# P·V of the sampled tokens with the cached values as the stationary operand, two matmuls a step, in place of one block and a turn back

## The chip, the cores and the metric

One core of one Trainium2 chip runs the whole program. The metric is the device time of one execution in microseconds; lower is better. The engines are TensorE (PE, with its weight loads shown apart as PEld), VectorE (DVE), ScalarE (ACT), GpSimd (POOL) and the DMA queues of SyncE (SP).

## What is computed

One decoder layer, in fp32, for 1024 prompt tokens and 8 sampled tokens, each sampled token with its own cache of keys and values. The mixer has 12 attention heads in 3 groups with dilations 1, 4 and 16. What the change touches is the attention of the sampled tokens. For each of the 8 sequences, each group and each of its 4 heads of 64 columns:

```python
kgat = jnp.take(kc, idxc, axis=1)          # up to 128 strided rows of the cache, and the own key
vgat = jnp.take(vc, idxc, axis=1)
s = jnp.einsum('nthd,ntkhd->nthk', qg, kgat).astype(jnp.float32) * SCALE
lse = jax.nn.logsumexp(s, axis=-1)
p = jnp.exp(s - lse[..., None])
outs.append(jnp.einsum('nthk,ntkhd->nthd', p.astype(vg.dtype), vgat))
```

The three groups are then merged by softmax weights; the kernel does this by one softmax over all three groups' scores of a token and head. The result (`o_a`, 256 columns a token) is projected with `w_proj_attn` and gated by `sigmoid(gate_a)`.

## The kernel before

**Tiling.** All activations are kept transposed, features on partitions and tokens along the free axis: 1032 tokens (`NT`), cut in three column tiles `tg` = 0, 1, 2 of 344 (`TG`). A fp32 product is made of three fast ones: both operands are split in a high and a low part, and `product3` (lines 474 to 479) does high·high, high·low and low·high. A *unit* is one 128 x 1024 block of weights: `unit` runs, for each `tg`, one `job` of 8 values of k with three matmuls each, 24 matmuls of 344 columns. `job` can take an `aside`: functions called just before a given k, which put foreign instructions into TensorE's order.

**Weights.** SP loads each unit's weights to `w_raw`; ACT copies the high part (`split`, L1005, to `w_hi`) once the unit two back is used up, DVE subtracts to get `w_lo` (L1500), and TensorE waits for `w_lo`.

**The stage in question.** In stage `ga` TensorE runs six units j = 0..5 of the gate A projection; ACT takes the tanh of each bank (L1235). The sampled tokens' attention runs between them: scores on DVE in j = 1 to 3, softmax in j = 3, then

- `sample_turn`, aside in (j, tg) = (4, 1) at k = 2: turns the probabilities `ssr` to `psA`; DVE copies them to `spT` (L1760 to L1762, semaphore `s_ptc`). `spT` holds, for each group, keys on partitions and 32 columns, one for each (sequence, head).
- `sample_pv`, aside in (4, 2) at k = 0: waits for `s_ptc` and for the 24 tiles of cached values `cv` (one for each sequence and group; 128 keys on partitions for the first two groups and 32 for the third, 256 columns: 4 heads of 64). For each tile one fp32 matmul takes **spT as the stationary operand** (32 columns) and streams 256 columns of `cv`; all 32 rows come out, although only the 4 of one sequence are wanted. Four sequences lie in four column strips of 32 of one bank (`psB`, `psC`). The own value rows (`svt`, 8 rows) go to `psA`. 27 matmuls, then `s_pv`.
- DVE copies the three results out (L1765 to L1767, `s_ov`).
- `sample_back`, aside in (5, 0) at k = 4: six transposes back to features on partitions (`s_ot`); DVE picks the wanted columns and adds the own part in 8 small operations (L1780) into the last 8 columns of `oaT`, each counting up `s_oa`.

**After it.** ACT waits for `s_oa` = 8 after the tanh of (5, 1) (L1242) and makes `oa_hi` of tile 2 (`oa_high(2)`, L1227), DVE `oa_lo` of tile 2 (`oa_low(2)`, L1722) and then the `w_lo` of the next unit. Stage `pa` (projection of `oaT`, 2 units of 2 values of k) waits for `oa_s` by tile; DVE multiplies its result by the gate (L1793, L1805). SP waits for `s_oa` (L414) before it loads `xs` and `grow` over the scratch space.

Of the kernel before, what the change touches and what calls it, by code (L numbers as in the profile page):

```python
# [12 lines left out]
ALU = mybir.AluOpType  # L13
ACT = mybir.ActivationFunctionType
F32 = mybir.dt.float32
# [4 lines left out]
P = 128  # L20
D = 1024
KD = D // P
SEQ = 1024
NS = 8
NT = SEQ + NS
TG = NT // 3
HD = 64
SLOTS = 4
GROUPS = 3
# [8 lines left out]
CKEYS = (128, 128, 32)  # L38
# [78 lines left out]
def build(nc, A, O):  # L117
    ctx = ExitStack()
    sem = lambda name: ctx.enter_context(nc.semaphore(name))
# [6 lines left out]
    X = R4 + RB  # L126
# [3 lines left out]
    def at(name, shape, dt, off):  # L130
        n = 4 if dt in (F32, F32R, I32) else 2
        for s in shape[1:]:
            n *= s
        assert off + n <= nc.sbuf_usable_end, (name, off, n)
        return nc.alloc_sbuf_tensor_at(name, shape, dt, offset=off), off + (n + 31) // 32 * 32

    with ctx:
# [4 lines left out]
        h_hi, _ = at("h_hi", [P, KD, NT], F32R, R[0])  # L142
        h_lo, _ = at("h_lo", [P, KD, NT], F32R, R[1])
        xn, _ = at("xn", [P, 8, D], F32, R[0])
# [3 lines left out]
        mb, _ = at("mb", [P, KD, NT], F32, R[2])  # L148
        m_hi, _ = at("m_hi", [P, KD, NT], F32R, R[2])
        a_hi, _o = at("a_hi", [P, FG, NT], F32R, R[2])  # L150
        a_lo, _ = at("a_lo", [P, FG, NT], F32R, _o)
        d_hi = [at(f"d_hi{i}", [P, 8 * P], F32R, R[2] + 2 * NT * 4 + 4096 * i)[0] for i in range(2)]
        d_lo = [at(f"d_lo{i}", [P, 8 * P], F32R, R[2] + (FG + 2) * NT * 4 + 4096 * i)[0] for i in range(2)]
        uv, _ = at("uv", [P, 8, NT], F32, R[3])
        ob_hi, _o = at("ob_hi", [P, 4, NT], F32R, R[3])
        ob_lo, _ = at("ob_lo", [P, 4, NT], F32R, _o)
        m_lo, _ = at("m_lo", [P, KD, NT], F32R, R[4])
        y2, _ = at("y2", [P, KD, NT], F32, R[4])
# [17 lines left out]
        oaT, _o = at("oaT", [P, 2, NT], F32, R[3])  # L176
# [36 lines left out]
        assert _o <= XEND and XEND - 3648 >= VTO, (_o, XEND)  # L213

        kq, _o = at("kq", [P, 2, 256], F32, X)
        ov, _ = at("ov", [P, 2, 256], F32, X)
        qz, _o = at("qz", [P, 2, 3, NS, 2], F32, _o)
        sst, _o = at("sst", [P, 2, 96], F32, _o)
        ssr, _o = at("ssr", [32, 320], F32, _o)
# [67 lines left out]
        sk_in = [sem(f"k_cache_landed{i}") for i in range(8)]  # L287
        sq_in = [sem(f"s_query_landed{i}") for i in range(3)]
        sv_in = sem("v_cache_landed")
        s_ov, s_ot = sem("s_pv_copied"), sem("s_pv_turned")  # L290
        s_qz, s_kq, s_sc, s_self, s_sst, s_rows, s_ssr, s_exp, s_pn, s_pt, s_ptc, s_pv, s_oa, s_nt, s_nc, s_out = [
            sem("s_" + s) for s in ("queries", "k_times_q", "scores", "self", "scores_out", "rows", "rows_out",
                                    "exp", "probs", "probs_turned", "probs_out", "pv", "o_out", "new_turned", "new_out",
# [33 lines left out]
        def _(sp):  # L327
# [83 lines left out]
            for i in range(2):  # L411
                load_ga(U0["gc"] + i, 6 + i)

            sp.wait_ge(s_oa, 8)  # L414
            sp.wait_ge(s_out, 48)
            sp.dma_start(xs[0:NS, :], x_s).then_inc(xr_in[8], 16)
            sp.dma_start(grow[:], A["g_mix_post"][0:1, :].broadcast_to([P, D])).then_inc(row_in, 16)
# [50 lines left out]
        def _(pe):  # L468
            mm = nc.tensor.matmul

            def turn(out, in_):
                k = in_.shape[0]
                return nc.tensor.transpose(out, in_, ident[0:k, 0:k])  # L473
# [320 lines left out]
                    ins = turn(psA[0:NS, 96 + 32 * g:128 + 32 * g], ssr[:, 288 + 8 * g:296 + 8 * g])  # L794
                ins.then_inc(s_pt, 1)

            def sample_pv():


                pe.wait_ge(s_ptc, 3)  # L800
                pe.wait_ge(sv_in, 16 * 24)
                for q, ps in ((0, psB), (1, psC)):
                    for g in range(GROUPS - 1):
                        for c in range(4):
                            mm(ps[32 * c:32 * c + 32, 0:256], spT[:, g, :], cv[:, 3 * (4 * q + c) + g, :],
                               start=(g == 0), stop=False)
                for q, ps in ((0, psB), (1, psC)):
                    for c in range(4):
                        mm(ps[32 * c:32 * c + 32, 0:256], spT[0:32, 2, :], cv[0:32, 3 * (4 * q + c) + 2, :],
                           start=False, stop=True)  # L810
                for g in range(GROUPS):
                    ins = mm(psA[0:32, 256:512], spT[0:NS, 3 + g, :], svt[:, g, 1, :], start=(g == 0), stop=(g == 2))
                ins.then_inc(s_pv, 1)

            def sample_back():

                pe.wait_ge(s_ov, 3)
                for q in range(2):
                    for p in range(2):
                        c = 256 * q + P * p  # L820
                        turn(psT[0][:, c:c + P], ov[:, q, P * p:P * p + P])
                for p in range(2):
                    ins = turn(psT[1][:, 32 * p:32 * p + 32], ssr[:, P * p:P * p + P])
                ins.then_inc(s_ot, 1)

            ASIDE_GA = {(4, 1): {2: sample_turn}, (4, 2): {0: sample_pv}, (5, 0): {4: sample_back}}

            for j in range(6):
                u = U0["ga"] + j

                def after(b, tg, j=j):
                    sample_step(j, tg)
                    merge_step(1, j, tg)
                unit(u, M0["ga"] + j, u % 2, 8, h_hi, h_lo, after=after,
                     aside=lambda tg, j=j: ASIDE_GA.get((j, tg)))
            for j in range(2):
                u = U0["pa"] + j
                unit(u, M0["pa"] + 4 * j, u % 2, 2, oa_hi, oa_lo, before=lambda tg: pe.wait_ge(oa_s, tg + 1))
# [158 lines left out]
        def _(act):  # L997
# [232 lines left out]
            for j in range(6):  # L1230
                for tg in range(3):
                    if (j, tg) == (4, 0):
                        act.wait_ge(s_kq, 24)
                    act.wait_ge(full[tg], M0["ga"] + j + 1)
                    fn(ga[:, j, tgc[tg]], bank[tg][:, 0:TG], ACT.Tanh, scale=0.5).then_inc(free[tg], 1)  # L1235
                    if (j, tg) == (3, 2):
                        act.wait_ge(s_ssr, 1)
                        fn(ssr[:, 0:312], ssr[:, 0:312], ACT.Exp, scale=SCALE, bias=stat[0:32, 53:54],
                           accum_out=stat[0:32, 54:55]).then_inc(s_exp, 1)
                    merge_in(1, j, tg)  # L1240
                    if (j, tg) == (5, 1):
                        act.wait_ge(s_oa, 8)  # L1242
                        oa_high(2)
                split_in(U0["ga"], 0, 0, j, M0["ga"] + j + 1)
                if j == 4:
                    oa_high(0)
                    oa_high(1)
# [242 lines left out]
        def _(dve):  # L1490
            v = nc.vector
# [249 lines left out]
            for j in range(6):  # L1741
                for kk in range(max(8 * j - 8, 0), min(8 * j, 24)):
                    if kk == 2:
                        merge_sum(1)
                    k_scores(kk)
                if j == 3:
                    dve.wait_ge(s_self, 1)
                    v.tensor_copy(sst[0:NS, 1, :], psB[0:NS, 0:96]).then_inc(s_sst, 1)
                    dve.wait_ge(s_rows, 1)
                    dve.wait_ge(masks_s, 2)  # L1750
                    st.link(v.tensor_copy(ssr[:, 0:288], psC[0:32, 0:288]))
                    st.link(v.tensor_tensor(ssr[:, 288:312], psC[0:32, 288:312], smask[:].rearrange("p g n -> p (g n)"), ALU.add))
                    st.link(v.reduce_max(stat[0:32, 55:56], ssr[:, 0:312], mybir.AxisListType.X))
                    v.tensor_scalar(stat[0:32, 53:54], stat[0:32, 55:56], -SCALE, None, ALU.mult).then_inc(s_ssr, 1)
                    dve.wait_ge(s_exp, 1)
                    st.link(v.reciprocal(stat[0:32, 56:57], stat[0:32, 54:55]))
                    v.tensor_scalar(ssr[:, 0:312], ssr[:, 0:312], stat[0:32, 56:57], None, ALU.mult).then_inc(s_pn, 1)
                    lo_in(U0["ga"], 0, 0, j)
                    dve.wait_ge(s_pt, 1)
                    v.tensor_copy(spT[:, 0:2, :].rearrange("p g n -> p (g n)"), psA[:, 0:64]).then_inc(s_ptc, 1)  # L1760
                    v.tensor_copy(spT[0:32, 2, :], psA[0:32, 64:96]).then_inc(s_ptc, 1)
                    v.tensor_copy(spT[0:NS, 3:6, :].rearrange("p g n -> p (g n)"), psA[0:NS, 96:192]).then_inc(s_ptc, 1)  # L1762
                if j == 4:
                    dve.wait_ge(s_pv, 1)
                    v.tensor_copy(ov[:, 0], psB[:, 0:256]).then_inc(s_ov, 1)  # L1765
                    v.tensor_copy(ov[:, 1], psC[:, 0:256]).then_inc(s_ov, 1)
                    v.tensor_copy(ssr[:, 0:256], psA[0:32, 256:512]).then_inc(s_ov, 1)  # L1767
                if j == 5:
                    oa_low(0)
                    oa_low(1)  # L1770
                    dve.wait_ge(s_ot, 1)
                    st.link(v.tensor_copy(sst[:, 0, 0:64], psT[1][:, 0:64]))
                    for p in range(2):
                        for q in range(2):
                            for e in range(2):

                                hd, at_n = slice(HD * e, HD * e + HD), SEQ + 4 * q
                                first = P * (2 * q + p) + 16 * q + 2 * p + e
                                own = 32 * p + 16 * q + 2 * p + e
                                v.tensor_tensor(oaT[hd, p, at_n:at_n + 4], psT[0][hd, first:first + 109:36],  # L1780
                                                sst[hd, 0, own:own + 13:4], ALU.add).then_inc(s_oa, 1)
                    oa_low(2)
                if j != 3:
                    lo_in(U0["ga"], 0, 0, j)
# [393 lines left out]
```

## Time and profile before

| | us |
|---|---|
| device time, median of the runs shown | 1582.84 |
| lowest of them | 1582.22 |
| the profiled execution | 1582.84 |
| its span, first to last instruction | 1580.9 |
| TensorE matmuls busy in the span | 1538.7 (97%) |
| TensorE weight loads busy | 1494.2 (95%) |
| DVE busy | 543.8 (34%) |
| ACT busy | 492.0 (31%) |
| POOL busy | 141.4 (9%) |

The profile is of one execution. Matmuls overlap: a dense one of 344 columns lasts 0.32 us in its row but the next one starts after 0.157 us, so the distance between starts tells more than the durations. A timeline row merges neighbouring instructions of one kind ("x16") and gives the start of the first and the time until the end of the last. "psB<-cv,spT 128*32 128x256" reads: output to `psB`, moving operand `cv` of 128 partitions x 256 elements, stationary operand `spT` of 128 rows * 32 columns. The granted clock is that of TensorE as a share of 2.4 GHz.

### The profile page before, as it was taken

To read this page: it belongs to the slowest core of one execution; us is meant where nothing else is said; L and a number is where in the kernel's file an instruction comes from. 1 tells how busy PE (TensorE), PEld (TensorE's weight loads), DVE (VectorE), ACT (ScalarE), POOL (GpSimd) and SP (SyncE) were. 2 spreads that over 40 slices of the span, in tenths; PEclk is the share of its full clock that TensorE was granted. 3 is DMA by queue.
4 is the path that set the end of the run, shared out by engine and by line. 5 is a ranking of instruction groups with operands and counts; after the bars stand their busy time and mean duration, and the time that the engine had idled before them with its cause. 6 is when DMAs were issued, how large, how long until landed. Compare 5 with 4: busy or idle time off the path is not lost.

```text
span 1580.9 us, 23134 instructions
## 1 busy us (share of the span) xinstructions
PE 1538.7 (97%) x9881; PEld 1494.2 (95%) x9881; DVE 543.8 (34%) x1016; ACT 492.0 (31%) x951; POOL 141.4 (9%) x172
## 2 busy tenths in 40 slices
PE   5999999999999999999999999999999999999995
PEld 5999999899998999998789999999999999999995
DVE  6104551332214336654652231132122213122236
ACT  5215543443224422336662111211111211121123
POOL 1000000000000025240001101100100110010014
PEclk9999999999999999999999999999999999999998
DMA  6111112100112025134422111111111111111102
GB/s 201 41 53 41 41 41 83 41 28 28 41 41 84 28 83 187 55 107 167 141 80 80 41 54 41 54 41 47 48 52 43 43 51 46 48 42 53 41 27 108
DMA packets 127169, 101.50 MB, mean 64 GB/s; under 512 B 4632, under 2 KB 114208, under 8 KB 127072
## 3 DMA queue, kind: packets, MB, share of 16 engines
q1 hardware_dynamic: 124208, 91.67, 18.7%
q0 software_dynamic: 2720, 7.89, 1.6%
q8 instruction: 75, 1.23, 0.3%
q10 hardware_dynamic: 144, 0.52, 0.1%
q14 instruction: 22, 0.18, 0.0%
HBM read 92.34 MB, written 7.73 MB: 63 GB/s over the span
## 4 chain that ended last, share of the span: by engine, by line
PE 92%; DVE 4%; POOL 1%; issue 1%; DMA 1%; ACT 1%; SPq 0%; ACTq 0%; DVEq 0%; POOLq 0%
PE bank L894 31%; PE bank L477 11%; PE bank L479 10%; PE bank L478 10%; PE bank L902 5%; PE bank L904 5%; PE bank L903 5%; PE psT L473 3%; PE psC L664 1%; PE bank L864 1%; PE bank L863 1%; PE bank L862 1%; PE psA L664 1%; POOL cv L2098 1%; PE psB L624 1%
## 5 line engine op out<-in xcount | busy, mean ns | idle before, releaser
L894 PE MATMUL bank<-f_hi,w_hi 128*128 128x384 f32 (+1 forms) x1056 | 338.6, 321 | 0.2 <-DVE w_lo L1500 0.2
L894 PE MATMUL bank<-f_hi,w_lo 128*128 128x384 f32 (+1 forms) x1056 | 337.8, 320 | 0.0
L894 PE MATMUL bank<-f_lo,w_hi 128*128 128x384 f32 (+1 forms) x1056 | 337.4, 320 | 0.0
L477 PE MATMUL bank<-h_hi,w_hi 128*128 128x344 f32 x1008 | 331.4, 329 | 1.6 <-DVE h_lo L1513 1.4
L1500 DVE TENSOR_TENSOR w_lo<-w_raw,w_hi 128x1024 fp32r<-128x1024 f32 x138 | 169.0, 1225 | 473.7 <-ACT w_hi L1424 226.6
L479 PE MATMUL bank<-h_hi,w_lo 128*128 128x344 f32 x1008 | 322.1, 320 | 0.0
L478 PE MATMUL bank<-h_lo,w_hi 128*128 128x344 f32 x1008 | 321.9, 319 | 0.0
L894 PEld LDWEIGHTS bank<-f_hi,w_hi 128*128 128x128 f32 x1056 | 198.5, 188 | 0.8 <-DVE w_lo L1500 0.5
L894 PEld LDWEIGHTS bank<-f_lo,w_hi 128*128 128x128 f32 x1056 | 198.5, 188 | 0.0
L894 PEld LDWEIGHTS bank<-f_hi,w_lo 128*128 128x128 f32 x1056 | 198.5, 188 | 0.0
L477 PEld LDWEIGHTS bank<-h_hi,w_hi 128*128 128x128 f32 x1008 | 190.0, 189 | 6.3 <-issue 5.0
L478 PEld LDWEIGHTS bank<-h_lo,w_hi 128*128 128x128 f32 x1008 | 189.7, 188 | 0.0
L479 PEld LDWEIGHTS bank<-h_hi,w_lo 128*128 128x128 f32 x1008 | 189.7, 188 | 0.0
L904 PE MATMUL bank<-a_hi,w_lo 128*128 128x384 f32 (+1 forms) x480 | 153.8, 320 | 0.0
L903 PE MATMUL bank<-a_lo,w_hi 128*128 128x384 f32 (+1 forms) x480 | 153.5, 320 | 0.0
L902 PE MATMUL bank<-a_hi,w_hi 128*128 128x384 f32 (+1 forms) x480 | 153.5, 320 | 0.0
L2124 POOL TENSOR_TENSOR a_lo<-sg,a_hi 128x384 fp32r<-128x384 f32 (+1 forms) x66 | 61.6, 934 | 776.7 <-ACT a_hi L1339 776.7
L1424 ACT ACTIVATE w_hi<-w_raw 128x1024 fp32r<-128x1024 f32 x58 | 61.0, 1052 | 202.6 <-PE bank L904 202.6
L1876 DVE TENSOR_TENSOR y<-y,bank 128x384 f32<-128x384 f32 (+1 forms) x120 | 61.1, 510 | 114.6 <-PE bank L904 114.6
L1339 ACT ACTIVATE a_hi<-sg 128x384 fp32r<-128x384 f32 (+1 forms) x66 | 32.5, 492 | 204.9 <-DVE sg L1868 204.9
L902 PEld LDWEIGHTS bank<-a_hi,w_hi 128*128 128x128 f32 x480 | 90.3, 188 | 0.0
L904 PEld LDWEIGHTS bank<-a_hi,w_lo 128*128 128x128 f32 x480 | 90.1, 188 | 0.0
(412 smaller groups left out, 1845.9 us busy)
## 6 DMA issues: line engine op xcount, KB each, us to landing
w_raw<-in_w_in SPq DMA_DIRECT2D x42, 512.0 KB, 3.9
w_raw<-in_w_out SPq DMA_DIRECT2D x24, 512.0 KB, 3.8
w_raw<-in_w_gate SPq DMA_DIRECT2D x23, 512.0 KB, 3.9
w_raw<-in_w_up SPq DMA_DIRECT2D x23, 512.0 KB, 4.0
w_raw<-in_w_down SPq DMA_DIRECT2D x22, 512.0 KB, 3.5
xin<-in_x_prompt SPq DMA_DIRECT2D x8, 512.0 KB, 7.7
xn<-in_x_prompt SPq DMA_DIRECT2D x8, 512.0 KB, 4.8
out_y_prompt<-xn SPq DMA_DIRECT2D x8, 512.0 KB
```

What stands on the lines that cost most here:

```text
L473: return nc.tensor.transpose(out, in_, ident[0:k, 0:k])
L477: mm(out[:, 0:TG], w_hi[par][:, ws], hi[:, k, tgc[tg]], start=first, stop=False)
L478: mm(out[:, 0:TG], w_hi[par][:, ws], lo[:, k, tgc[tg]], start=False, stop=False)
L479: return mm(out[:, 0:TG], w_lo[par][:, ws], hi[:, k, tgc[tg]], start=False, stop=last)
L894: ins = mm(out[:, 0:NG[tg]], w[par][:, ws], x[tg][:, k, :], start=(k == 0 and w is w_hi and x is f_hi), stop=(k == KD - 1 and w is w_lo))
L902: mm(out[:, 0:NG[tg]], hi[:, ws], a_hi[:, k, tgf[tg]], start=(k == 0), stop=False)
L903: mm(out[:, 0:NG[tg]], hi[:, ws], a_lo[:, k, tgf[tg]], start=False, stop=False)
L904: ins = mm(out[:, 0:NG[tg]], lo[:, ws], a_hi[:, k, tgf[tg]], start=False, stop=(k == kc - 1))
L1424: fn(w_hi[j % 2][:], w_raw[j % 2][:], ACT.Copy).then_inc(w_hi_s, 1)
L1500: v.tensor_tensor(w_lo[par][:], w_raw[par][:], w_hi[par][:].bitcast(F32), ALU.subtract).then_inc(w_lo_s, 1)
L1876: v.tensor_tensor(part, part, src[:, 0:NG[tg]], ALU.add).then_inc(free[tg], 1)
L2124: g_.tensor_tensor(a_lo[:, j, tgf[tg]], sg[:, tgf[tg]], a_hi[:, j, tgf[tg]].bitcast(F32), ALU.subtract).then_inc(ff_l, 1)
```

## The change

The roles are swapped. `sample_pv(c)` is now one of 27 steps of two fp32 matmuls (p = 0, 1: the two halves of 128 of the 256 value columns). In each, 128 columns of `cv` or `svt` are the **stationary** operand, and the moving operand is only the wanted probabilities: 2 columns (the two heads of that half) for a cache tile, 16 for the own rows. The result comes out with features on partitions, all in the first 32 columns of `psB`, so nothing has to be turned back. One start flag (the first own-row matmul) and one stop flag (the last) bound the accumulation.

The steps lie one at each k: the three own-row steps in (4, 1) at k = 5, 6, 7; the 24 cache steps at k = 0 to 7 of (4, 2), (5, 0) and (5, 1). `sample_turn` stays at (4, 1), k = 2. `sample_back`, the tile `ov` and the semaphores `s_ov` and `s_ot` go. DVE waits for `s_pv` in j = 5, between `oa_low(1)` and `oa_low(2)`, and copies twice from `psB` to `oaT`; `s_oa` ends at 2.

```diff
-            sp.wait_ge(s_oa, 8)
+            sp.wait_ge(s_oa, 2)
...
-            def sample_pv():
-                pe.wait_ge(s_ptc, 3)
-                pe.wait_ge(sv_in, 16 * 24)
-                for q, ps in ((0, psB), (1, psC)):
-                    for g in range(GROUPS - 1):
-                        for c in range(4):
-                            mm(ps[32 * c:32 * c + 32, 0:256], spT[:, g, :], cv[:, 3 * (4 * q + c) + g, :],
-                               start=(g == 0), stop=False)
-                for q, ps in ((0, psB), (1, psC)):
-                    for c in range(4):
-                        mm(ps[32 * c:32 * c + 32, 0:256], spT[0:32, 2, :], cv[0:32, 3 * (4 * q + c) + 2, :],
-                           start=False, stop=True)
-                for g in range(GROUPS):
-                    ins = mm(psA[0:32, 256:512], spT[0:NS, 3 + g, :], svt[:, g, 1, :], start=(g == 0), stop=(g == 2))
-                ins.then_inc(s_pv, 1)
-
-            def sample_back():
-                pe.wait_ge(s_ov, 3)
-                for q in range(2):
-                    for p in range(2):
-                        c = 256 * q + P * p
-                        turn(psT[0][:, c:c + P], ov[:, q, P * p:P * p + P])
-                for p in range(2):
-                    ins = turn(psT[1][:, 32 * p:32 * p + 32], ssr[:, P * p:P * p + P])
-                ins.then_inc(s_ot, 1)
-
-            ASIDE_GA = {(4, 1): {2: sample_turn}, (4, 2): {0: sample_pv}, (5, 0): {4: sample_back}}
+            def sample_pv(c):
+                if c == 0:
+                    pe.wait_ge(s_ptc, 3)
+                for p in range(2):
+                    if c < GROUPS:
+                        out = psB[:, 16 * p:16 * p + 16].rearrange("k (n e) -> k n e", e=2)
+                        w = spT[0:NS, 3 + c, :].rearrange("k (n s) -> k n s", s=4)[:, :, 2 * p:2 * p + 2]
+                        mm(out, svt[:, c, 1, P * p:P * p + P], w, start=(c + p == 0), stop=False, skip_group_check=True)
+                        continue
+                    if c == GROUPS and p == 0:
+                        pe.wait_ge(sv_in, 16 * 24)
+                    kk = c - GROUPS
+                    n, g = kk // 3, kk % 3
+                    ck = CKEYS[g]
+                    ins = mm(psB[:, 16 * p + 2 * n:16 * p + 2 * n + 2], cv[0:ck, kk, P * p:P * p + P],
+                             spT[0:ck, g, 4 * n + 2 * p:4 * n + 2 * p + 2], start=False,
+                             stop=(kk == 23 and p == 1), skip_group_check=True)
+                    if kk == 23 and p == 1:
+                        ins.then_inc(s_pv, 1)
+
+            PV_AT = [(4, 1, 5), (4, 1, 6), (4, 1, 7)] + [(j, tg, k) for j, tg in ((4, 2), (5, 0), (5, 1)) for k in range(KD)]
...
-                        act.wait_ge(s_oa, 8)
+                        act.wait_ge(s_oa, 2)
...
-                if j == 4:
-                    dve.wait_ge(s_pv, 1)
-                    v.tensor_copy(ov[:, 0], psB[:, 0:256]).then_inc(s_ov, 1)
-                    v.tensor_copy(ov[:, 1], psC[:, 0:256]).then_inc(s_ov, 1)
-                    v.tensor_copy(ssr[:, 0:256], psA[0:32, 256:512]).then_inc(s_ov, 1)
                 if j == 5:
                     oa_low(0)
                     oa_low(1)
-                    dve.wait_ge(s_ot, 1)
-                    st.link(v.tensor_copy(sst[:, 0, 0:64], psT[1][:, 0:64]))
-                    for p in range(2):
-                        for q in range(2):
-                            for e in range(2):
-                                hd, at_n = slice(HD * e, HD * e + HD), SEQ + 4 * q
-                                first = P * (2 * q + p) + 16 * q + 2 * p + e
-                                own = 32 * p + 16 * q + 2 * p + e
-                                v.tensor_tensor(oaT[hd, p, at_n:at_n + 4], psT[0][hd, first:first + 109:36],
-                                                sst[hd, 0, own:own + 13:4], ALU.add).then_inc(s_oa, 1)
+                    dve.wait_ge(s_pv, 1)
+                    for e in range(2):
+                        hd = slice(HD * e, HD * e + HD)
+                        v.tensor_copy(oaT[hd, :, SEQ:NT], psB[hd, 0:32].rearrange("d (p n e) -> d p n e", p=2, e=2)[:, :, :, e]
+                                      ).then_inc(s_oa, 1)
                     oa_low(2)
```

## Rows read from the trace of the kernel before

**Rows 1.** The page: chain that ended last, by engine and by line

```profile
PE 92%; DVE 4%; POOL 1%; issue 1%; DMA 1%; ACT 1%; SPq 0%; ACTq 0%; DVEq 0%; POOLq 0%
PE bank L894 31%; PE bank L477 11%; PE bank L479 10%; PE bank L478 10%; PE bank L902 5%; PE bank L904 5%; PE bank L903 5%; PE psT L473 3%; PE psC L664 1%; PE bank L864 1%; PE bank L863 1%; PE bank L862 1%; PE psA L664 1%; POOL cv L2098 1%; PE psB L624 1%
```

**Rows 2.** Timeline of TensorE, `sample_pv`: start us, us, engine, line, operation

```profile
628.45 0.31 PE L479 MATMUL bank<-h_hi,w_lo 128*128 128x344 f32 x1
...
629.16 1.07 PE L805 MATMUL psB<-cv,spT 128*32 128x256 f32 x16 [0.40 <-DMA cv<-in_cache_win]
...
633.56 0.32 PE L478 MATMUL bank<-h_lo,w_hi 128*128 128x344 f32 x1
```

**Rows 3.** Timeline of TensorE around `sample_back`

```profile
638.90 0.32 PE L479 MATMUL bank<-h_hi,w_lo 128*128 128x344 f32 x1
...
640.09 0.32 PE L478 MATMUL bank<-h_lo,w_hi 128*128 128x344 f32 x1
```

**Rows 4.** Timeline, three transposes between dense matmuls

```profile
293.10 0.32 PE L479 MATMUL bank<-h_hi,w_lo 128*128 128x344 f32 x1
...
293.26 0.49 PE L473 MATMUL psT<-ident,pr 128*128 128x128 f32 x3
...
293.75 0.32 PE L478 MATMUL bank<-h_lo,w_hi 128*128 128x344 f32 x1
```

**Rows 5.** Timeline, twelve fp32 passes of the prompt's P·V

```profile
296.59 0.31 PE L479 MATMUL bank<-h_hi,w_lo 128*128 128x344 f32 x1
...
296.75 0.78 PE L664 MATMUL psA<-vtok,prT 128*128 128x64 f32 x6
...
298.30 0.32 PE L478 MATMUL bank<-h_lo,w_hi 128*128 128x344 f32 x1
```

**Rows 6.** Timeline around L775, then L775 by source line

```profile
611.60 0.32 PE L479 MATMUL bank<-h_hi,w_lo 128*128 128x344 f32 x1
...
611.85 0.46 PE L775 MATMUL psB<-qz,sqkv 128*8 128x16 f32 x12
...
612.24 0.42 PE L477 MATMUL bank<-h_hi,w_hi 128*128 128x344 f32 x1
...
L775 PE MATMUL psB<-qz,sqkv x12: 176/176/183, 611.8 to 612.1; 128*8 128x16 f32 x12
```

**Rows 7.** Weight loads: L624, `vw` by tile, then their timeline

```profile
L624 PEld LDWEIGHTS psB<-qk x64: 187/187/188, 286.8 to 550.0; 64*128 64x128 f32 x64
...
L473 PEld LDWEIGHTS psA<-ident,vw x4: 133/136/137, 234.3 to 234.5; 8*128 8x128 f32 x4
...
234.33 0.32 PEld L473 LDWEIGHTS psA<-ident,vw 8*128 8x128 f32 x4 [0.21 <-issue]
```

**Rows 8.** Timeline of DVE, TensorE and ACT up to the next stage

```profile
626.01 0.24 DVE L1762 COPY spT<-psA 8x96 f32<-8x96 f32 x1
...
627.19 0.32 PE L477 MATMUL bank<-h_hi,w_hi 128*128 128x344 f32 x1
...
645.79 0.46 ACT L1235 ACTIVATE ga<-bank 128x344 f32<-128x344 f32 x1 [3.31 <-PE bank L479]
...
646.15 0.77 ACT L1227 ACTIVATE oa_hi<-oaT 128x688 fp32r<-128x688 f32 x1
...
649.92 1.05 ACT L1005 ACTIVATE w_hi<-w_raw 128x1024 fp32r<-128x1024 f32 x1
...
651.00 1.22 DVE L1500 TENSOR_TENSOR w_lo<-w_raw,w_hi 128x1024 fp32r<-128x1024 f32 x1 [3.18 <-ACT w_hi L1005]
```

**Rows 9.** Busy us by stretch with clock (PEclk), then timeline of TensorE there

```profile
core 0: us, PE busy (x) PEld busy (x) DVE busy (x) ACT busy (x) POOL busy (x), PEclk, DMA share, GB/s
...
17.00:24.00 7.00, 3.95 (x20) 3.60 (x21) 6.82 (x12) 5.73 (x12) 1.28 (x3) 0.55 0.97 291
...
23.24 0.49 PE L478 MATMUL bank<-h_lo,w_hi 128*128 128x344 f32 x1
...
23.53 0.49 PE L479 MATMUL bank<-h_hi,w_lo 128*128 128x344 f32 x1
```

More of the change, by code:

```diff
@@ L215, in build @@
         kq, _o = at("kq", [P, 2, 256], F32, X)
-        ov, _ = at("ov", [P, 2, 256], F32, X)
         qz, _o = at("qz", [P, 2, 3, NS, 2], F32, _o)
@@ L289, in build @@
         sv_in = sem("v_cache_landed")
-        s_ov, s_ot = sem("s_pv_copied"), sem("s_pv_turned")
         s_qz, s_kq, s_sc, s_self, s_sst, s_rows, s_ssr, s_exp, s_pn, s_pt, s_ptc, s_pv, s_oa, s_nt, s_nc, s_out = [
@@ L828, in _, with pv_aside @@
+            PV_AT = [(4, 1, 5), (4, 1, 6), (4, 1, 7)] + [(j, tg, k) for j, tg in ((4, 2), (5, 0), (5, 1)) for k in range(KD)]
+            def pv_aside(j, tg):
+                steps = {k: (lambda c=c: sample_pv(c)) for c, (a, b, k) in enumerate(PV_AT) if (a, b) == (j, tg)}
+                if (j, tg) == (4, 1):
+                    steps[2] = sample_turn
+                return steps
             for j in range(6):
@@ L834, in _ @@
                 unit(u, M0["ga"] + j, u % 2, 8, h_hi, h_lo, after=after,
-                     aside=lambda tg, j=j: ASIDE_GA.get((j, tg)))
+                     aside=lambda tg, j=j: pv_aside(j, tg))
             for j in range(2):
```

## The prediction, made before the changed kernel ran

> **What bounds the kernel now.** I read the page's chain first: 92% of the span is TensorE work and its leading lines are the matmul streams [rows 1]. So an edit is worth what it adds to or takes from TensorE's own instruction stream, unless it makes TensorE wait. Then the timeline of TensorE around the sampled tokens' P·V. The dense stream (`product3`, 344 columns) starts a matmul every 0.157 us: from 633.56 to 638.90 there are 34 intervals [rows 2, 3]. I price each interruption of that stream by one rule: take the slot at which the next dense matmul was due, take the start of the *second* dense matmul after the interruption, subtract, and subtract one slot of 0.157. The second is used because the first one after an interruption is itself followed 0.24 to 0.27 us later, not 0.157.
>
> `sample_pv`: last dense start 628.45, so the next was due at 628.61; second start afterwards 633.56 [rows 2]. 633.56 − 628.61 − 0.157 = 4.79 us, of which 0.40 is a wait for the cached values. `sample_back`: last dense start 638.90, due 639.06, second afterwards 640.09 [rows 3]: 0.87 us. Together **5.66 us of TensorE** on the path.
>
> **Removed.** 27 matmuls of `sample_pv`, 6 transposes, three DVE copies out of PSUM, one more copy and eight tiny adds. Only the TensorE part counts: nothing waits for DVE's part but the chain to `oa_hi(2)`, costed below. Credit 5.66 us. The 0.40 us wait is rightly in the credit: the new own-row groups come before the wait for the cache, so TensorE gets there later than 628.61 by about 2 us, after the values have landed.
>
> **Added: how many instructions.** 27 groups (3 own-row, 24 cache) of two fp32 matmuls. An fp32 matmul appears as two passes with a weight load each: L805 is 8 matmuls on `psB` and 16 records [rows 2]. So 54 matmuls are 108 passes, 4 in a group, and every pass loads a stationary tile 128 columns wide, where before it was 32. The moving side shrinks from 256 columns to 2 (16 for own rows). Streaming becomes nothing; loading becomes everything. The question is what four 128-wide loads cost when wedged between dense matmuls.
>
> **Price of a group without change of row tile** (16 groups, 128 keys). Nearest rows: three transposes with 128-wide loads: due 293.26, second dense start 293.75, loss 0.33 us [rows 4]. Twelve fp32 passes in the prompt's P·V, 128-wide loads, only 64 moving columns: due 296.75, second dense start 298.30, loss 1.39 us [rows 5]. Slope (1.39 − 0.33)/9 = 0.118 us per load, so four cost 0.33 + 0.118 = **0.45 us**. 16 × 0.45 = 7.2 us.
>
> **Price of a group that changes the row tile** (8 groups of 32 keys and 3 of 8 own rows). A 64-row, 128-wide load still lasts 187 ns [rows 7], so I let fewer rows save nothing. But a change of tile shape costs extra. The twelve passes of L775 (8-column loads) were due at 611.757 and began at 611.85, so 0.09 us on entry. Their last pass starts at 611.85 + 0.46 − 0.176 = 612.134, and the dense stream resumes at 612.24, 0.106 us later [rows 6], although nothing in that pass takes 0.1 us; I round that to 0.12 for leaving. 0.45 + 0.09 + 0.12 = **0.66 us**. 11 × 0.66 = 7.26 us.
>
> The Trainium skill, "TensorE: Matmul & The Clock Gate", section "LDWEIGHTS (loading the stationary operand)", says that a load lasts its column count divided by 1.2, in ns, whatever the rows. By that rule alone, with 107 ns a load, 27 groups of four would cost an estimated 11.6 us, net +5.9 us; the 0.21 us for changing the tile shape isn't in it. The rows agree with the rule on the load and add the shape change, and I go by the rows. The rule speaks against this change: it makes the 128-wide operand the stationary one.
>
> **Waits that move.** The own-row groups now need `spT` at (4,1), k=5; `sample_pv` needed it only at (4,2), k=0. The last copy to `spT` ends at 626.25 and TensorE is at k=5 at 627.19 [rows 8]: 0.9 us to spare, no stall; `sample_turn` stays where it was. If that cover were gone TensorE would stall by the excess alone.
>
> The result is now complete only in the last k of (5,1) instead of at 633. Queued behind on DVE: two copies (under 0.25 us each, as L1762), `oa_low(2)`, then `lo_in(5)`; on ACT, behind `wait_ge(s_oa, 2)`: `oa_high(2)`, the tanh of (5,2), the w_hi split; on SP nothing earlier than `xs` and `grow`, which follow weight loads already held back by `w_lo`. The pass that signals is issued 3 dense matmuls (0.47 us) before (5,1) ends. ACT does not look at `s_oa` before it has done the tanh of (5,1), 0.46 us, which in turn waits for that job's end [rows 8]. Two copies fit in 0.47 + 0.46 = 0.93 us, so `oa_high(2)` still follows the tanh directly, as it did at 646.15. `oa_low(2)` follows within 2 us, while (5,2) keeps TensorE busy 24 × 0.157 = 3.8 us, and tile 2 of unit pa is wanted a further 0.94 later. Nothing added. If the copies were a microsecond late, `oa_low(2)` still is in time.
>
> What follows is tied to TensorE: the w_hi split at 649.92 waits for the end of (5,2), the w_lo at 651.00 for it, the products after that [rows 8]. So a delay of TensorE reaches the end in full, with no slack to swallow it.
>
> **Sum.** +7.2 + 7.26 − 5.66 = +8.8 us. The profiled execution lasted 1582.84 us with a span of 1580.9 and is the median of the runs shown, so the forecast is 1582.84 + 8.8 = **1591.6 us**, +0.56%: slower, but within 2% (about what a measurement of this kernel can tell from no change).
>
> **Bounds.** Low: every group at the transposes' 0.33 us, 27 × 0.33 = 8.9, net +3.3, 1586.1 us. High: every group pays the shape change and 0.05 more for the second column range, 27 × 0.71 = 19.2, net +13.5, 1596.3 us.
>
> **Rivals.**
> *A, the forecast* (loads of 107 to 118 ns bound each pass): 70%.
> *B, fast loads.* Four transposes of 8 rows had 128-wide loads and finished four loads within 0.32 us, (0.32 − 0.13)/3 = 0.063 apart [rows 7]. If few moving columns allow that pace, a group costs 0.25, with shape change 0.46: 16 × 0.25 + 11 × 0.46 = 9.1, net +3.4, 1586.2 us. Against: those were transposes, and the fp32 matmuls of [rows 5] did not reach it. 10%.
> *C, not slower.* The pass follows the moving width, not the stationary one. L775 with 16 moving columns runs at (0.46 − 0.176)/11 = 0.026 us per pass [rows 6]; at that pace a group costs 0.10, with shape change 0.31: 16 × 0.10 + 11 × 0.31 = 5.0, net −0.6, 1582.2 us. It decides if a group costs under 5.66/27 = 0.21 us. For: the moving side does shrink to 2 columns. Against: L775's stationary side was 8 wide too, and [rows 4, 5] have the same 128-wide load but 128 and 64 moving columns at nearly one pace. 5%.
> *D, no overlap.* With 2-column passes each load waits until the matmul before it has left the array: 0.106 us (as between the end of L775 and the dense stream) on top of 0.118, four times: 0.90 us a group, 24.3, net +18.6, 1601.5 us. Against: L775's small passes show no such gap. 8%.
> *E, the clock falls.* The groups cut TensorE's dense share from (4,2) to (5,1) to 0.47 of 0.92 to 1.13 us. In the start phase with TensorE busy 3.95 of 7 us the granted clock was 0.55, toward the 1.2 GHz level, and a dense matmul took 0.29 us [rows 9]. If all 24 steps ran so: 24 × 3 × 0.13 = 9.4 us more for the dense part alone, 1601 us. Against: before that fall the engine had been truly idle, and here it is loading all the time. 7%. The Trainium skill, "TensorE: Matmul & The Clock Gate", Part 1, makes the low level the default that activity lifts; whether loads with two columns count as activity no row here shows.
>
> **Range.** 1585.5 to 1597: it holds A within its bounds and B (80%), and leaves out C, D and E. A alone: 1588 to 1596. Faster by over 2%: 0.01. Slower by over 2% (above 1614.5) would need D and E together: 0.02. Within 2%: 0.97.
>
> **What would show it.** TensorE between (4,1) k=5 and the end of (5,1) longer by 14.5 us minus the two blocks taken out; groups of 4 passes with starts 0.11 apart; group loss 0.45 at 128 keys and 0.66 at 32; no TensorE wait for `spT` or the cache; `oa_high(2)` following ACT's tanh directly; clock 1.00 in 625 to 665. Wrong if a group costs under 0.3 or over 0.8 us, if the dense matmuls slow to 0.29, or if a stage after 670 changes length.

## The result, and the profile after

The changed kernel takes 1592.72 us (median of 5 runs, 1592.64 to 1593.27) against 1582.84 us for the median shown before. The ratio to the kernel before is **1.0057, 95% interval 1.0045 to 1.0069**: slower by 0.57%, within 2%. The kernel before ran five times beside it, at 1582.22, 1582.84, 1584.68, 1584.70 and once 1905.31 us, and the ratio leaves the last one out and goes by the median of the other four, 1583.8 us. So the change costs 8.9 us by that median and 9.9 us by the one shown before; the forecast was +8.8, 1591.6 us.

The page of the changed kernel (span; matmuls and weight loads, DVE, ACT, POOL busy; chain that ended last, by engine):

```profile
span 1590.3 us, 23220 instructions
...
PE 1549.5 (97%) x9929; PEld 1504.5 (95%) x9929; DVE 542.0 (34%) x1006; ACT 492.3 (31%) x951; POOL 141.5 (9%) x172
...
PE 94%; DVE 3%; ACT 1%; issue 1%; DMA 1%; SPq 0%; POOL 0%; ACTq 0%; DVEq 0%
```

The span grew from 1580.9 to 1590.3 us, TensorE's busy time by 10.8 us; the chain is still TensorE's.

Where the 9.4 us lie can be read off without any pricing rule. The stretch from `sample_turn` to the first matmul of stage `pa` holds the same dense matmuls in both kernels. Its ends, before and then after:

```profile
625.31 0.42 PE L473 MATMUL psA<-ident,ssr 32*128 32x32 f32 x6
...
649.37 0.32 PE L477 MATMUL bank<-oa_hi,w_hi 128*128 128x344 f32 x1
```

```profile
625.16 0.42 PE L471 MATMUL psA<-ident,ssr 32*128 32x32 f32 x6
...
658.68 0.32 PE L475 MATMUL bank<-oa_hi,w_hi 128*128 128x344 f32 x1
```

It took 24.05 us and now takes 33.52, **9.47 us more**. From the first matmul of `pa` to the end of the span it is 931.5 us before and 931.6 after: everything that follows kept its length.

Timeline of TensorE in the changed kernel (lines are two lower than before: the dense stream is L475 to L477). First a step with a tile of 128 keys, then one with 32 keys:

```profile
630.51 0.32 PE L477 MATMUL bank<-h_hi,w_lo 128*128 128x344 f32 x1
...
630.67 0.50 PE L810 MATMUL psB<-spT,cv 128*128 128x2 f32 x4
...
631.28 0.32 PE L476 MATMUL bank<-h_lo,w_hi 128*128 128x344 f32 x1
...
632.36 0.31 PE L477 MATMUL bank<-h_hi,w_lo 128*128 128x344 f32 x1
...
632.61 0.60 PE L810 MATMUL psB<-spT,cv 32*128 32x2 f32 x4
...
633.40 0.32 PE L476 MATMUL bank<-h_lo,w_hi 128*128 128x344 f32 x1
```

Read by the rule of the prediction. 128 keys: due 630.667, second dense start 631.28, loss 0.46 us. 32 keys: due 632.517, second dense start 633.40, loss 0.73 us. The 0.09 us between due and start of the first pass (632.61) is the entry into another row tile, as in [rows 6]. The own-row steps:

```profile
626.88 0.32 PE L477 MATMUL bank<-h_hi,w_lo 128*128 128x344 f32 x1
...
627.12 0.61 PE L803 MATMUL psB<-spT,svt 8*128 8x16 f32 x4
...
627.94 0.32 PE L476 MATMUL bank<-h_lo,w_hi 128*128 128x344 f32 x1
```

Due 627.037, second dense start 627.94: 0.75 us. Over all 27 steps of the trace the means are 0.741 us (own rows), 0.726 (32 keys) and 0.448 (128 keys): 3 x 0.741 + 8 x 0.726 + 16 x 0.448 = **15.2 us added**, where [rows 2, 3] gave 5.66 us back: 9.5 us net, as the stretch above shows. The number of passes was as counted (24 cache tiles x 2 halves x 2 passes; count, ns min/median/max, starts, shapes):

```profile
L810 PE MATMUL psB<-spT,cv x96: 165/251/267, 630.7 to 654.2; 128*128 128x2 f32 x64, 32*128 32x2 f32 x32
```

The hand-over to the next stage: DVE's two copies, then ACT's tanh, `oa_high(2)` and the next w_hi split:

```profile
L1767 DVE COPY oaT<-psB x2: 167/172/178, 654.4 to 654.6; 64x16 f32<-64x16 f32 x2
...
655.11 0.46 ACT L1233 ACTIVATE ga<-bank 128x344 f32<-128x344 f32 x1 [7.72 <-PE bank L477]
...
655.47 0.77 ACT L1225 ACTIVATE oa_hi<-oaT 128x688 fp32r<-128x688 f32 x1
...
659.23 1.05 ACT L1003 ACTIVATE w_hi<-w_raw 128x1024 fp32r<-128x1024 f32 x1
```

DVE copies at 654.4 and 654.6, ACT starts its own tanh at 655.11 and `oa_high(2)` directly after it at 655.47, as at 646.15 in [rows 8]. Before, the w_hi split that follows unit (5,2) started at 649.92 [rows 8]; now it starts at 659.23, 9.3 us later.

Busy us and granted clock over the 27 steps, changed kernel (columns as in [rows 9]; the clock is the last but two):

```profile
627.10:655.00 27.90, 27.90 (x191) 25.58 (x191) 3.14 (x5) 3.65 (x6) 0.00 (x0) 1.00 0.11 34
```

It stays at the 2.4 GHz level through all 27 steps. The 24 executions of the changed kernel on record lie between 1591.91 and 1593.53 us, with a granted clock of 0.995 or more over the whole span, so none of them lost the clock here.

### The profile page after: what moved, and what is told of

It is laid out like the page before. It is cut to its first block, busy times and chain, and to the rows that moved or that the text cites. A ratio compares the mean times of both kernels' runs of the same rounds, so it can differ in the third digit from the quotient of the medians.

```text
span 1590.3 us, 23220 instructions
## 1 busy us (share of the span) xinstructions
PE 1549.5 (97%) x9929; PEld 1504.5 (95%) x9929; DVE 542.0 (34%) x1006; ACT 492.3 (31%) x951; POOL 141.5 (9%) x172
## 4 chain that ended last, share of the span: by engine, by line
PE 94%; DVE 3%; ACT 1%; issue 1%; DMA 1%; SPq 0%; POOL 0%; ACTq 0%; DVEq 0%
PE bank L892 31%; PE bank L475 12%; PE bank L477 11%; PE bank L476 11%; PE bank L900 5%; PE bank L902 5%; PE bank L901 5%; PE psT L471 3%; PE psC L662 1%; PE bank L862 1%; PE bank L861 1%; PE bank L860 1%; PE psA L662 1%; PE psB L810 1%; DMA xin<-in_x_prompt 1%
## 5 line engine op out<-in xcount | busy, mean ns | idle before, releaser
L475 PE MATMUL bank<-h_hi,w_hi 128*128 128x344 f32 x1008 | 333.6, 331 | 1.6 <-DVE h_lo L1511 1.4
L477 PE MATMUL bank<-h_hi,w_lo 128*128 128x344 f32 x1008 | 322.0, 319 | 0.0
L475 PEld LDWEIGHTS bank<-h_hi,w_hi 128*128 128x128 f32 x1008 | 190.0, 188 | 6.0 <-issue 4.6
L477 PEld LDWEIGHTS bank<-h_hi,w_lo 128*128 128x128 f32 x1008 | 189.5, 188 | 0.0
```

Source lines behind the costliest of these rows:

```text
L475: mm(out[:, 0:TG], w_hi[par][:, ws], hi[:, k, tgc[tg]], start=first, stop=False)
L477: return mm(out[:, 0:TG], w_lo[par][:, ws], hi[:, k, tgc[tg]], start=False, stop=last)
```

## Experiments

The theory: each fp32 pass costs a weight load of 128 columns, about 0.11 us (the expectations below reckon with 0.107; the traces give 0.112); a change of row tile costs 0.27 us a step; leaving and re-entering the dense stream costs next to nothing beyond that; what TensorE loses here reaches the end in full. Stage lengths below are from the first own-row pass to the first matmul of `pa`: 658.68 − 627.12 = 31.56 us in the changed kernel.

### e3: no 32-row tiles

```diff
+                    if g == 2:
+                        kk, g = kk - 1, 1
                     ck = CKEYS[g]
```

> The changed kernel, but each tile of 32 keys is replaced by the tile of 128 keys before it (the third group's values are not used: part of the result is wrong); the number of steps, loads and columns is the same and only the change of row tile is gone. Theory: 8 groups fall from 0.73 to 0.45 us, the stage is 2.2 us shorter. Rival 'row count' (fewer rows load faster, and the change costs more than 0.27): over 3 us or under 1 us.

1590.32 us, one execution. The step that had 32 rows, now 128:

```profile
632.83 0.32 PE L477 MATMUL bank<-h_hi,w_lo 128*128 128x344 f32 x1
...
632.98 0.50 PE L812 MATMUL psB<-spT,cv 128*128 128x2 f32 x4
...
633.59 0.32 PE L476 MATMUL bank<-h_lo,w_hi 128*128 128x344 f32 x1
```

Due 632.987, second dense start 633.59, loss 0.446 us instead of 0.73. The stage is 29.38 us, 2.18 less: 0.27 us a step for going to a 32-row tile and back. By itself this run can't tell a dear change from a dear 32-row pass; e1 below can, since its 32-row passes in a row start 0.112 us apart, like those of 128 rows. So the 0.27 us is the change in and out, and the rows themselves save nothing.

### e4: 23 of the 24 cache steps left out

```diff
-... if (a, b) == (j, tg)}
+... if (a, b) == (j, tg) and (c < 3 or c == 26)}
```

> The changed kernel with 23 of the 24 cache steps left out (the three own-row steps and the last cache step stay, with all waits and copies; the sampled tokens' attention lacks nearly all of its values). Theory (a delay of TensorE in this stage reaches the end in full): 16 groups at 0.45 and 7 at 0.73 are gone, 12.3 us, so 1592.7 - 12.3 = 1580.4 us. Rival 'slack later' (the next stages, where TensorE waits for DVE, swallow part): 1583 to 1588 us.

1580.67 us (1579.73 to 1581.16), ratio to the kernel before 0.9979 (0.9969 to 0.9988). The stage is 19.36 us, 12.20 less; the median of the whole kernel is 12.05 less. (The profiled executions are 11.4 us apart in span, because in this one the stage began 0.8 us later.) The sharper evidence is what follows the stage: from the first matmul of `pa` to the end of the span it is 931.6 us here, and 931.5 to 931.6 us in all fourteen traces of this case. Removed step time arrives at the end one for one; the next stages swallow nothing.

### e5 and e6: 64 and 256 streamed columns instead of 2

```diff
+                    if ck == P:
+                        mm(psC[:, 0:64], cv[0:ck, kk, P * p:P * p + P], spT[:, 0:2, :], start=True, stop=True)
+                        continue
```

(e6: `psC[:, 0:256]` and `cv[:, kk, :]` as the moving operand.)

> The changed kernel, but the 16 steps of 128 keys stream 64 columns of probabilities instead of 2 and write to an unused bank (their part of the result is left out). Theory (the load bounds a pass as long as streaming takes less than 0.107 us): a group costs 0.45 to 0.50 us as with 2 columns, only its last pass is longer. Rival 'moving width': 62 more columns a pass at the 0.83 ns a column seen for 256 columns add 0.05 us a pass, 0.21 us a group.

> As e5_move64 with 256 streamed columns (cached values against cached values; that part of the result is left out). Theory: streaming takes 0.214 us a pass (the prompt's scores and the own rows of the kernel before run at that pace) and now bounds it: a group costs 4 x 0.214 = 0.86 plus 0.05 to 0.1 us, 0.45 more than with 2 columns, 7 us over 16 groups. If load and streaming did not overlap, it would be 4 x 0.32 = 1.28 us a group.

They took 1593.31 and 1598.75 us, one execution each. Timeline of TensorE, e5 and then e6, one step of 128 keys each:

```profile
632.62 0.32 PE L477 MATMUL bank<-h_hi,w_lo 128*128 128x344 f32 x1
...
632.78 0.55 PE L811 MATMUL psC<-spT,cv 128*128 128x64 f32 x4
...
633.38 0.32 PE L476 MATMUL bank<-h_lo,w_hi 128*128 128x344 f32 x1
```

```profile
630.46 0.32 PE L477 MATMUL bank<-h_hi,w_lo 128*128 128x344 f32 x1
...
630.62 1.03 PE L811 MATMUL psC<-cv 128*128 128x256 f32 x4
...
631.64 0.32 PE L476 MATMUL bank<-h_lo,w_hi 128*128 128x344 f32 x1
```

e5: due 632.777, second dense 633.38, loss 0.45 us; the stage is 659.87 − 628.31 = 31.56 us, the same as with 2 columns to the last digit. 32 times as many columns cost nothing. e6: due 630.617, second dense 631.64, loss 0.87 us; the stage is 38.30 us, 6.74 more, 0.42 a step. Four passes of 256 columns at 0.214 us are 0.86 us: there streaming is the bound, and the loads hide under it. So a pass costs the larger of load and streaming, and the moving width (the prediction's case C) plays no part up to 64 columns. Where streaming takes over was not measured; from 0.112 us a load and 0.214 us for 256 columns, an estimate is 134 columns.

### e1 and e2: one block, with full and half stationary width

```diff
-            steps = {k: (lambda c=c: sample_pv(c)) for c, (a, b, k) in enumerate(PV_AT) ...}
+            if (j, tg) == (4, 2):
+                return {0: sample_block}       # own rows, 32-key tiles, 128-key tiles
```

> The swapped matmuls of the changed kernel, all 27 steps in one aside at (4,2), k=0, ordered own rows, then the 8 tiles of 32 keys, then the 16 of 128 keys. Theory (the price is 108 loads of 128 columns at 0.107 us, plus 0.27 us for each change of row tile): 11.6 us for the loads, one change in and one out instead of eleven, so the block costs about 11.9 us against 15.3 us for the 27 scattered groups; device time about 3.4 us below the changed kernel, 1589.3. Rival 'interruption' (what costs is leaving and re-entering the dense stream 27 times, a pass itself only 0.03 us): the block costs 3 to 4 us, device time 1581. Rival 'no difference': 1592.7.

> As e1_block, but each cache matmul takes only 64 of its 128 stationary columns (the other half of the values of each pair of heads is left out, so part of the sampled tokens' result is missing). Theory: 96 of the 108 loads take half as long, 0.053 instead of 0.107, so the block is 5.1 us shorter than e1_block's, if the matmul's moving side of 2 columns and a fixed floor of 0.03 us set nothing. Rival 'moving width': the same length as e1_block. Rival 'fixed cost a pass': the same length as e1_block too.

(Both edits also move the wait for the cache to the first cache step of the new order and the stop flag to the last; e9 to e12 do the same.)

e1 took 1598.79 us (1598.5 to 1599.57), ratio 1.0095 (1.0078 to 1.0112): *slower* than the scattered version by 6 us, where 3.4 us less were expected. Timeline of TensorE: own rows, then the 96 cache passes, then the dense stream:

```profile
628.65 1.51 PE L803 MATMUL psB<-spT,svt 8*128 8x16 f32 x12
...
630.01 18.90 PE L810 MATMUL psB<-spT,cv 32*128 32x2 f32 x96
...
648.77 0.63 PE L475 MATMUL bank<-h_hi,w_hi 128*128 128x344 f32 x1
```

96 passes from 630.01 to 648.77 are 0.195 us each on average, not 0.107. The clock says why (columns as above), and then the passes by source line before and after it fell (count, ns min/median/max, starts):

```profile
631.00:632.00 1.00, 1.00 (x11) 1.00 (x11) 0.00 (x0) 0.00 (x0) 0.00 (x0) 1.00 0.00 0
632.00:633.00 1.00, 1.00 (x7) 1.00 (x6) 0.00 (x0) 0.00 (x0) 0.00 (x0) 0.50 0.00 0
...
L810 PE MATMUL psB<-spT,cv x16: 246/246/246, 630.1 to 631.8; 32*128 32x2 f32 x16
...
L810 PE MATMUL psB<-spT,cv x75: 348/352/374, 632.5 to 648.3; 128*128 128x2 f32 x63, 32*128 32x2 f32 x12
```

At 632 us, inside the block, the granted clock fell from 1.00 to 0.50, the 1.2 GHz level. Before it fell, TensorE had done nothing but 128-column loads with 16 or 2 streamed columns since 628.65. The passes started 0.112 us apart before (1.7 us over 15 intervals, 0.113 as rounded here) and 0.213 us after (15.8 over 74). The low level lasted to 652.5, so the first dense matmuls after the block ran at it too. The busy columns show nothing of it: 1.00 of 1.00 on both sides.

The block of the kernel before is as long a stay away from the dense stream, and it kept the clock:

```profile
629.00:633.50 4.50, 4.34 (x55) 2.36 (x56) 0.09 (x1) 0.26 (x1) 0.00 (x0) 1.00 0.01 4
```

Its passes load 32 columns and stream 256. It differs from e1 in both, so it doesn't say which of the two matters; it does say that leaving the dense stream for 4 us isn't enough by itself.

e2 took 1590.02 us, one execution. A stretch before and one after its clock fell, then the passes at the low level by source line:

```profile
631.20:634.20 3.00, 3.00 (x52) 2.98 (x52) 0.00 (x0) 0.00 (x0) 0.00 (x0) 1.00 0.02 5
...
634.30:644.40 10.10, 10.10 (x65) 10.09 (x65) 0.00 (x0) 0.00 (x0) 0.00 (x0) 0.50 0.00 0
...
L810 PE MATMUL psB<-spT,cv x40: 246/246/246, 634.5 to 638.7; 128*64 128x2 f32 x40
```

In the 3.0 us at full clock 52 passes are in flight, about 0.058 us each where the full-width pass takes 0.112. At the low level they start 0.107 us apart (4.2 over 39 intervals) where e1's start 0.213 apart. At either level half the width costs half the time, so the price does follow the stationary width, and both rivals, 'moving width' and 'fixed cost a pass', fall. The blocks' totals can't be compared, since the clock fell at different points in them.

### e9 and e10: fewer, larger asides

```diff
+            # e9
+            BLOCKS = {(4, 1, 5): [0, 1, 2], **{(4, 2, 2 * i): SHORT[2 * i:2 * i + 2] for i in range(4)},
+                      **{(5, i // 4, 2 * (i % 4)): LONG[2 * i:2 * i + 2] for i in range(8)}}
+            # e10
+            BLOCKS = {(4, 2, 0): [0, 1, 2] + SHORT, (5, 0, 0): LONG[:8], (5, 1, 0): LONG[8:]}
```

> The changed kernel with the same 27 steps in 13 asides: the 3 own-row steps together, the 8 tiles of 32 keys in 4 pairs, the 16 of 128 keys in 8 pairs. Loads are the same 108, changes of row tile fall from 11 to 5. Theory (0.107 a load, 0.27 a change of row tile, nothing for being an interruption): 108 x 0.107 + 13 x 0.02 + 5 x 0.27 = 13.2 us against 15.3, so 2.1 us below the changed kernel, 1590.6; clock 1.00 throughout, since no aside is longer than 1.6 us. Rival 'interruption': 27 asides become 13, at 0.3 us each 4 us less, 1588.5. Rival 'clock': asides of 0.9 to 1.6 us already lower the clock, over 1594.

> The 27 steps in three blocks, one at k=0 of (4,2), (5,0) and (5,1): 44, 32 and 32 loads, 4.7 + 0.27, 3.4 and 3.4 us at full clock, with 3.8 us of dense matmuls between them. If the granted clock stays at 1.00: 108 x 0.107 + 0.3 = 11.9 us, 1589.3. If it falls inside a block as in e1_block (there 3.4 us after the first of the 2-column passes), what is left of the block runs at half pace and the dense matmuls after it too: each stretch of 6.8 us at half clock costs 3 us or more, 1592 to 1602. I expect it to fall in the first block at least.

e9: 1608.47 us (1604.25 to 1610.42), ratio 1.0154 (1.0132 to 1.0176), the slowest of all. A pair of 32-key tiles early on, and a pair of 128-key tiles later:

```profile
634.96 1.05 PE L810 MATMUL psB<-spT,cv 32*128 32x2 f32 x8
...
635.94 0.42 PE L475 MATMUL bank<-h_hi,w_hi 128*128 128x344 f32 x1
...
641.36 1.70 PE L810 MATMUL psB<-spT,cv 128*128 128x2 f32 x8
...
642.92 0.63 PE L475 MATMUL bank<-h_hi,w_hi 128*128 128x344 f32 x1
```

```profile
630.00:636.20 6.20, 6.20 (x43) 5.52 (x42) 0.00 (x0) 0.46 (x1) 0.00 (x0) 1.00 0.01 3
...
636.50:670.30 33.80, 33.80 (x137) 33.42 (x136) 3.27 (x6) 4.31 (x7) 0.00 (x0) 0.50 0.05 16
```

The first pair takes 635.94 − 634.96 = 0.98 us (eight loads and part of the shape change), the later one 642.92 − 641.36 = 1.56 us without a shape change. That is 0.195 a pass, but the first interval after dense matmuls is a short one; the others are 0.213 us, as in e1. The clock fell at 636.3 and stayed down until 670.4, past the last pair (done at 666.91): the dense matmuls between the pairs ran at that level too and did not lift it. The stage is 45.62 us, 14.1 more than the changed kernel's, in an execution of 1606.70 us. The expectation's rival 'clock' (over 1594) is what came.

e10: 1597.17 us (1596.79 to 1599.41), ratio 1.0088 (1.0072 to 1.0105), inside the band expected. Second and third block, with the clock in two stretches between and in them:

```profile
640.28 3.63 PE L810 MATMUL psB<-spT,cv 128*128 128x2 f32 x32
...
643.77 0.41 PE L475 MATMUL bank<-h_hi,w_hi 128*128 128x344 f32 x1
...
645.10:648.30 3.20, 3.20 (x13) 3.20 (x12) 0.00 (x0) 0.00 (x0) 0.00 (x0) 0.50 0.38 115
...
648.60:651.80 3.20, 3.20 (x30) 3.20 (x28) 0.00 (x0) 0.46 (x1) 0.00 (x0) 1.00 0.03 5
...
649.18 4.39 PE L810 MATMUL psB<-spT,cv 128*128 128x2 f32 x32
...
653.43 0.63 PE L475 MATMUL bank<-h_hi,w_hi 128*128 128x344 f32 x1
```

The second block ran at full clock: 32 passes in 643.77 − 640.28 = 3.49 us, 0.109 each; without the short first interval the starts lie 0.112 us apart. The third started at full clock and fell on the way: 4.25 us. The clock fell in or just after each block (at 634.8, 645.0 and 651.9) and came back between them and after the last. (The expectation puts e1's fall 3.4 us after its first 2-column pass; that pass started at 630.01, so it was 2.0 us.)

### e11 and e12: is it the streamed columns?

As e1, but 92 of the 96 cache passes stream 64 (e11) or 16 (e12) columns to the unused bank `psC`; the last four still stream 2.

> e1_block with 64 streamed columns in each cache pass instead of 2, to an unused bank (that part of the result is left out): the same instructions, the same loads, the same busy rows. Theory (the clock fell in e1_block because next to nothing was streamed): the granted clock stays at 1.00, a pass takes 0.107 us and the block 12 us; 1589.3. Rival (the clock follows the kind of work, loads against matmuls, or the length of the gap in the dense stream): it falls as in e1_block, 1598.8.

> As e11_block64 with 16 streamed columns. Theory: between e1_block and e11_block64; 16 columns are an eighth of what the load lasts, and I expect the clock to fall, 1598.8. If it stays at 1.00, 1589.3.

1598.61 us and 1599.7 us, one execution each, with e1_block's 1598.79. e11's clock:

```profile
628.00:632.00 4.00, 4.00 (x32) 3.79 (x31) 0.00 (x0) 0.46 (x1) 0.00 (x0) 1.00 0.28 104
...
636.00:640.00 4.00, 4.00 (x21) 4.00 (x20) 0.00 (x0) 0.00 (x0) 0.00 (x0) 0.50 0.00 0
```

Before it fell, at 634.7, e11's passes also started 0.112 us apart. In e12 it fell at 633.7. Neither 16 nor 64 columns a pass kept the clock up. My explanation for e1, that next to nothing was streamed, falls in the form in which I put it; that more columns, or wider passes still, would hold it was not tried.

### e7 and e8: the kernel before, two small edits

```diff
-            ... (4, 2): {0: sample_pv} ...
+            ... (4, 2): {2: sample_pv} ...
+            # e8 only: each group to its own column strip, added up by DVE after the turn
+                    ins = mm(psA[32 * g:32 * g + 32, 256:512], spT[0:NS, 3 + g, :], svt[:, g, 1, :], start=True, stop=True)
```

> The kernel before with its P.V block two values of k later, at (4,2), k=2. Theory: the wait for the cached values (0.40 us of the block's 4.79) is gone, since TensorE comes there 0.94 us later; the block costs 4.3 us, the kernel is 0.4 us faster than before. Rival: the wait was for something that moves along, no change.

> As e7_before_late, and the own rows of the three groups go to three column strips of psA at the same time instead of one after the other into one strip; DVE adds the three after the turn back (three more small operations while TensorE works). Theory: six passes one after the other at 0.214 us become two rounds of three at once, 1.28 us becomes about 0.5; with the wait gone the kernel is 1.2 us faster than before, 10.8 us faster than the changed one. Rival: the added DVE work delays oa_hi(2) and the next stage, no gain over e7.

e7: 1582.9 us, ratio 0.9997 (0.9988 to 1.0006). Its last dense start before the block, own rows, second dense start after:

```profile
630.38 0.31 PE L479 MATMUL bank<-h_hi,w_lo 128*128 128x344 f32 x1
...
633.38 1.46 PE L812 MATMUL psA<-svt,spT 8*32 8x256 f32 x6
...
635.02 0.32 PE L478 MATMUL bank<-h_lo,w_hi 128*128 128x344 f32 x1
```

Due 630.537, 635.02: the block costs 4.33 us, 0.46 less than the 4.79 of [rows 2]; the wait for the cached values is gone. The stretch from `sample_turn` to `pa` is 23.59 us against 24.05. In the device time that gain is smaller than the interval, so it is shown in the trace alone.

e8: 1581.63 us, ratio **0.9989 (0.998 to 0.9998)**. Own rows:

```profile
633.46 0.60 PE L812 MATMUL psA<-svt,spT 8*32 8x256 f32 x6
```

Six passes with 256 columns end 0.60 us after they begin instead of 1.46, three strips working at once. A second, smaller gain was not expected: `sample_back` now turns 96 rows where it turned 32, and costs 0.63 us instead of 0.87, about what a change to a 32-row tile costs in e3. The stretch from `sample_turn` to `pa` is 22.47 us, 1.6 less than before. That is the best version here with the whole result: 1.0 us under the kernel before and 11.1 us under the changed one. It is a gain of a tenth of a percent and just clear of its interval.

## Why the prediction was right, point by point

- **The credit of 5.66 us** was read off the trace, and e7 confirms its one soft part: 0.4 us of it was a wait for the cache. In the changed kernel no pass of L810 waits for a DMA.
- **108 passes, each with a 128-wide load**: 96 passes for the cache and 12 for the own rows, as counted. The price per pass, interpolated at 0.118 from [rows 4, 5], measured 0.112 (e1 before its clock fell, e10's second block). The group price of 0.45 us was right: 0.448 measured, which is four passes and nothing beside them.
- **A change of row tile** was the term that was mis-sized: put at 0.09 + 0.12 = 0.21 us, measured 0.27 (e3: 2.18 us over 8 steps). 8 x (0.73 − 0.66) + 3 x (0.74 − 0.66) = 0.8 us, about the whole difference between 8.8 and 9.5 us net. From 9.5 to the 8.9 or 9.9 of the medians is the spread of the kernel before's own executions. Entering costs 0.09 us as put, leaving about 0.18, not 0.12. L775 in [rows 6], from which I took both, has all 128 rows and 8 columns: that is a change of the column shape, not of the row tile, so the price of the one was used for the other, and that its entry fits is luck.
- **Waits**: no stall at `spT`, none at the cache, `oa_high(2)` still directly behind ACT's tanh. DVE's copies took 172 ns each and were done before ACT began.
- **One for one to the end**: e4, 12.20 us in the stage and 12.05 in the kernel; after the stage 931.5 to 931.6 us in every trace.
- **Case B** (transposes' load pace) did not occur: 0.112 against 0.063. **Case C** (moving width) is refuted by e5 and, with e1, by e2. **Case D** (drain after each pass) would have given 0.22 us a pass.
- **Case E, the clock, was underestimated.** It got 7% because [rows 9] showed a fall only where TensorE had been idle. e1, e2 and e9 to e12 show that TensorE can be busy without a gap and still lose the clock. The forecast held because this order, one step at each k, keeps it. No row that the prediction read tells that order from the ones that lose the clock, so in this point it was lucky. The same instructions in pairs (e9) cost 16 us more. My price for case E, 9.4 us more, covered the dense matmuls alone; e9 shows that the passes themselves slow from 0.112 to 0.213 us as well, and its stage grew by 14.1 us. The Trainium skill, "TensorE: Matmul & The Clock Gate", Part 1, says that the gate goes by how busy the engine has recently been. e1 agrees that it is a gate with two levels, but the fall came with the matmul and load rows both full, so the busy share of a profile can't stand in for what the gate reads.

**What stays open.** Why pairs lose the clock and single steps don't, with the same loads and the same dense matmuls between them. e9 differs in three ways: eight passes stand in a row instead of four, its 32-key tiles come first and together (four pairs), and its own rows are one aside of 1.5 us. Which of them tips it isn't settled. It isn't chance: the four executions of e9 took 1604.25 to 1610.42 us, the 24 of the changed kernel at most 1593.53. Nor is what a pass would need for the clock to hold: 2, 16 and 64 streamed columns all lose it in a block, and the block of the kernel before, which keeps it, has 256 columns and narrower loads at once.

## What to carry to other kernels

The price of a small fp32 matmul is the larger of its weight load (0.112 us a pass for 128 stationary columns, whatever the rows, two passes a matmul) and its streaming (0.214 us for 256 columns), both at the full clock. Making the wide operand stationary to save streaming and a turn back therefore loses as soon as the loads cost more than what is saved: here 15.2 us for 5.7. Count loads before streamed columns. Each trip to another row tile adds 0.27 us, but each version with the whole result that sorted the small matmuls by tile shape (e1, e9, e10) also put them closer together, lost the clock and was slower.

Put such work between dense matmuls in small pieces, and look at the granted clock afterwards: a block of wide loads with 2 to 64 streamed columns dropped it to half while the busy rows were full. Fewer interruptions isn't a gain in itself: beyond its four passes an interruption costs nothing that these traces show, a lost clock 14 us (e9).

## What the hardware showed that I had not expected

- The granted clock fell to 0.50 with TensorE's matmul and load rows both full (e1: 632 us), also with 64 columns streamed in each pass (e11), and stayed there from 636.3 to 670.4 us with dense matmuls in between (e9).
- At the low level loads and streaming both take nearly twice as long: a dense matmul starts every 0.287 us instead of 0.157, a 128-column pass every 0.213 instead of 0.112, a 64-column pass every 0.107 instead of 0.058 (e1, e2).
- From 2 to 64 streamed columns the stage didn't change by 0.01 us (e5).
- Three matmuls on three 32-column strips of one bank run at the same time also with 8 rows each: 0.60 us against 1.46 (e8).
